# A two-block model on one core: the router's first scores taken tile by tile, and rows of U gathered two groups ahead of V

## The chip, the core and the metric

The kernel runs on one core of one Trainium2 chip. Its engines each run their own instruction stream: TensorE (PE, with its weight loads as PEld), VectorE (DVE), ScalarE (ACT), GpSimd (POOL) and SyncE (SP), and they wait for one another through semaphores. The metric is the device time of one execution in microseconds.

## The reference

The model is a block with two attention branches and a PEER layer, then two layers of a second block (gated linear attention beside latent attention). The change lies in the PEER layer and in the router ahead of it, for 256 tokens of width 1024:

```python
q = (hf @ wq).reshape(T, 8, 2, 128)                  # 8 heads, two halves each
sc = jnp.einsum('thpd,pnd->thpn', q, subkeys)        # 128 scores for each half
top_v, top_i = lax.top_k(sc, 16)
cand_v = top_v[:, :, 0, :, None] + top_v[:, :, 1, None, :]
best_v, best_j = lax.top_k(cand_v.reshape(T, 8, -1), 16)
ids = ...                                            # 128 rows of the tables for each token
gates = jax.nn.softmax(best_v, axis=-1)
a = jnp.einsum('td,ted->te', xb, jnp.take(u_tab, ids, axis=0))
w = gates * jax.nn.gelu(a, approximate=False)
y = jnp.einsum('te,ted->td', w, jnp.take(v_tab, ids, axis=0))
```

Each token takes 128 rows of U and the same 128 rows of V, each of 1024 float32 values. Both tables have 16384 rows and stay in HBM.

## The kernel before

**The PEER layer.** The tokens lie in two tiles of 128 (t = 0, 1). A *piece* is two heads of one tile, so there are 8 pieces. A piece has 32 row numbers for each token; 8 of them are a *group*, so there are 4 groups in a piece (GPP) and 32 in all. One gather is an indirect DMA that POOL issues: for each of the 128 partitions it fetches the row that this token wants, 512 KB. There are 256 gathers of U and 256 of V (`u_rows`, `v_rows`, both through L707). Rows of U go to 8 buffers (`urow`, half of the ring of weights), rows of V to 8 others (`vgat`). A row of U is used by one DVE instruction (L1786), which multiplies it with the token's activations and sums; this frees the buffer (`u_free`). After 8 rows ACT takes the gelu (L915), DVE multiplies with the gates (L1789), and ACT writes 8 diagonal matrices (L920). PE multiplies each diagonal with a row of V, two halves of 512 columns (L1317), into two banks that stay open for a whole tile; this frees the buffer of V (`v_free`).

**The order of the gathers.** `piece` (L724) issues for each group n the pairs U(n+1, s), V(n, s) for s = 0 to 7. So U runs one group ahead. The row numbers of a group are first copied to two small tiles (`stage_ids`, L711). U(n+1, s) waits until DVE has used U(n, s), V(n, s) until PE has used V(n-1, s).

**The selection.** For each piece DVE runs `best_halves` (16 best of each half), `best_pairs` (16 best of the sums) and `experts_and_gates` (row numbers and gates), for piece k+1 while piece k is gathered: one step after each of the first three groups; in the first piece the first step follows group 1, the other two group 2. ACT takes the exponentials of the gates (L910) between the last two.

**The router.** The order on PE and ACT is written out in `router_schedule` (L174). A job ("pq", ch) is the product with 512 columns of `peer_wq` (4 heads' halves), ("sc", t, ch) the scores of tile t against the subkeys from it; each takes whole PSUM banks, which `plan_banks` deals out in turn, and ACT empties them. Ahead of them the normalised rows of both tiles are transposed ("hT"). ("ada", 11) is the last of twelve products that spread a modulation vector over the partitions; DVE sums it first (`sum_ada`, L1531) and the product reads a tile of ones that lies in the space of `gates`. The first product, ch = 0, is made tile by tile (`tile_products`, L1117), so that it can begin while tile 1 is still normalised, but into banks that hold both tiles. Its scores feed the first selection, which ends in the first row numbers, for which POOL waits. The gathers also wait for the ring of weights: U(0, 0) for `sum_ada(11)`, U(0, 4) for ("pq", 1), V(0, 0) for ("pq", 2), V(0, 4) for ("pq", 3).

Ahead of the first selection DVE has this (L1773 to L1777):

```python
await_full(dve, ("ada", 11))
drained(dve, ("sc", 0, 0))
best_halves(0)
```

## Time and profile before

| | us |
|---|---|
| median of 3 runs | 1359.54 |
| lowest and highest | 1354.93, 1366.68 |
| the profiled execution | 1348.18 |
| its span in the trace | 1346.4 |
| DVE busy in the span | 645.3 (48%) |
| POOL busy in the span | 631.6 (47%) |
| PE busy in the span | 1074.0 (80%) |

The profiled execution is one of its own, and it is faster than each of the three timed runs. The gathers and their products fill the span from 262 to 1037 us. What lies ahead of them is the first block's attention and the router, and behind them the two layers of the second block. In rows of a timeline the first number is the start in us from the span's start and the second the duration in us.

### The profile page before, as it was taken

The page shows a single profiled execution, that of the slowest core. Times are in us where ns is not written, and L with a number is a line of the kernel's source. Part 1 is how long each engine was busy: PE and PEld are TensorE (multiplying, and loading weights), DVE is VectorE, ACT ScalarE, POOL GpSimd, SP SyncE. Part 2 cuts the span into 40 slices and gives each one's busy share as a digit, 9 for nine tenths or more (in the row PEclk, how much of TensorE's full clock was granted, in tenths as well). Part 3 has the DMA queues.
Part 4 walks back from the last instruction along what each step waited for, and adds up shares of the span by engine and source line. Part 5 has one row for each costly group of instructions (what it writes and reads, how often), then busy time and mean ns, then how long its engine had stood idle before and what let it go on. Part 6 is the DMA issues. An engine that isn't in the chain of part 4 may idle for free.

```text
span 1346.4 us, 11936 instructions
## 1 busy us (share of the span) xinstructions
PE 1074.0 (80%) x3367; PEld 544.1 (40%) x3367; DVE 645.3 (48%) x1463; ACT 269.2 (20%) x731; POOL 631.6 (47%) x653
## 2 busy tenths in 40 slices
PE   2899998997766667766776767766768999999988
PEld 2758655872222222222222222222224645555453
DVE  4534665557566465465555655564442133211530
ACT  3012231122011020110111311020111162113340
POOL 1400001177777777777777777777773001000000
PEclk9799999999999999999989799899999999799999
DMA  9985545499999999999999999999999543123300
GB/s 347 295 301 196 187 156 155 170 329 356 356 349 350 344 336 347 355 362 342 351 339 342 345 345 371 340 361 356 357 359 367 196 152 109 41 101 125 125 0 31
DMA packets 121589, 361.66 MB, mean 269 GB/s; under 512 B 13416, under 2 KB 16240, under 8 KB 121424
## 3 DMA queue, kind: packets, MB, share of 16 engines
q0 software_dynamic: 76000, 276.39, 56.6%
q1 hardware_dynamic: 42768, 82.97, 17.2%
q10 hardware_dynamic: 2784, 1.88, 0.5%
q8 instruction: 15, 0.25, 0.1%
q14 instruction: 22, 0.18, 0.0%
HBM read 360.15 MB, written 1.05 MB: 268 GB/s over the span
## 4 chain that ended last, share of the span: by engine, by line
PE 39%; POOL 21%; issue 17%; DMA 13%; ACT 5%; DVE 3%; POOLq 1%; ACTq 0%; DVEq 0%
POOL wring L707 21%; PE bank L1126 13%; DMA wring<-in_peer_v,small 9%; PE bank L1136 8%; PE bank L1317 5%; PE bank L1117 3%; DMA wring<-in_peer_u,small 3%; PE bank L1183 2%; PE bank L1197 1%; DVE R L1561 1%; DMA xrow<-in_x 1%; PE bank L1220 1%; PE bank L1474 1%; PE bank L1473 1%; PE bank L1306 1%
## 5 line engine op out<-in xcount | busy, mean ns | idle before, releaser
L1317 PE MATMUL bank<-wring,hT 128*128 128x512 f32 x1024 | 525.2, 642 | 214.7 <-DMA wring<-in_peer_v,small 213.3
L1786 DVE CUSTOM_DVE_ANT_0 wring<-wring,hrow 128x1024 f32<-128x1024 f32 x256 | 310.0, 1225 | 287.5 <-DMA wring<-in_peer_u,small 287.3
L1317 PEld LDWEIGHTS bank<-wring,hT 128*128 128x128 f32 x1024 | 183.2, 197 | 556.4 <-issue 518.4
L707 POOL DMA_INDIRECT wring<-in_peer_u,small x256 | 283.9, 1109 | 96.4 <-issue 59.1
L707 POOL DMA_INDIRECT wring<-in_peer_v,small x256 | 283.9, 1109 | 80.2 <-issue 74.2
L1126 PE MATMUL bank<-wring,hT 128*128 128x512 f32 (+1 forms) x448 | 195.3, 593 | 0.0
L745 POOL TENSOR_SCALAR small<-small 128x2 f32<-128x2 f32 (+3 forms) x16 | 3.1, 194 | 386.5 <-ACTq L817 220.8
L1126 PEld LDWEIGHTS bank<-wring,hT 128*128 128x128 f32 x448 | 85.1, 192 | 101.5 <-issue 101.5
L915 ACT ACTIVATE small<-small 128x8 f32<-128x8 f32 x32 | 6.7, 209 | 580.7 <-DVE small L1786 580.7
L1136 PE MATMUL bank<-hT,wring 128*128 128x256 f32 x448 | 101.9, 388 | 0.9 <-DVE hT L1578 0.9
L1136 PEld LDWEIGHTS bank<-hT,wring 128*128 128x128 f32 x448 | 86.2, 194 | 15.4 <-issue 3.6
L920 ACT ACTIVATE hT<-const,small 128x128 f32<-128x128 f32 x256 | 78.3, 388 | 11.4 <-DVE small L1789 11.4
L1117 PE MATMUL bank<-hT,wring 128*128 128x128 f32 x384 | 45.9, 282 | 8.4 <-ACT hT L840 8.4
L1531 DVE SCALAR_TENSOR_TENSOR modb<-wring,small,modb 128x512 f32<-128x512 f32 x64 | 48.1, 751 | 7.2 <-DMA wring<-in_ada_w 3.6
L1117 PEld LDWEIGHTS bank<-hT,wring 128*128 128x128 f32 x384 | 44.8, 197 | 9.8 <-issue 6.8
L711 POOL COPY small<-ids 128x8 uint32 (+1 forms) x64 | 16.1, 251 | 37.7 <-DVEq L1765 31.5
L1856 DVE SCALAR_TENSOR_TENSOR R<-R,small,gains 128x128 f32<-128x128 f32 x4 | 1.4, 348 | 57.7 <-POOLq L751 57.7
L2016 DVE TENSOR_TENSOR xrow<-xrow,bank 128x512 f32<-128x512 f32 x8 | 5.5, 688 | 48.6 <-PE bank L1126 48.6
L1183 PE MATMUL bank<-wring,hT 128*128 128x512 f32 x64 | 28.2, 596 | 0.3 <-ACT hT L870 0.3
L840 ACT ACTIVATE hT<-bank 128x512 f32<-128x512 f32 x24 | 13.5, 595 | 70.9 <-PE bank L1105 61.4
L685 POOL DMA_DIRECT2D hrow<-in_na_rpb x8 | 5.5, 720 | 45.9 <-DVE rope L1606 45.9
L892 ACT ACTIVATE R<-R,small 128x256 f32<-128x256 f32 x32 | 16.0, 500 | 42.1 <-DVEq L1660 42.1
(249 smaller groups left out, 883.9 us busy)
## 6 DMA issues: line engine op xcount, KB each, us to landing
wring<-in_w_in SPq DMA_DIRECT2D x14, 2048.0 KB, 9.4
wring<-in_ada_w SPq DMA_DIRECT2D x8, 2048.0 KB, 11.0
wring<-in_w_out SPq DMA_DIRECT2D x6, 2048.0 KB, 11.1
wring<-in_ada_w SPq DMA_DIRECT2D x8, 1024.0 KB, 16.2
wring<-in_peer_wq SPq DMA_DIRECT2D x4, 2048.0 KB, 12.0
wring<-in_peer_u,small POOLq DMA_INDIRECT x256, 6.1
wring<-in_peer_v,small POOLq DMA_INDIRECT x256, 6.2
wring<-in_w_in SPq DMA_DIRECT2D x2, 1792.0 KB, 14.8
```

Source lines behind the costliest of these rows:

```text
L707: pool.indirect_dma_start(dst, None, table, bass.IndirectOffsetOnAxis(index, 0)).then_inc(landed, 16)
L711: chain.link(pool.tensor_copy(dst, ids[:, bass.ds(n * GROUP, GROUP)] if not isinstance(n, int) else ids[:, n * GROUP:(n + 1) * GROUP]))
L840: free(act.activation(hT[:, 4 * g:4 * g + 4, t * P:(t + 1) * P], quad(pb[:, :]), ACT.Copy), (kind, t, g))
L892: act.activation(Em[:, h % 2, qt, :], Tm[:, h % 2, qt, :], ACT.Exp, scale=-1.0, bias=accmin[:, i:i + 1], accum_out=rsum[:, qt, h:h + 1]).t ...
L920: act.activation(diag[:, b * GROUP + s, :], ident, ACT.Copy, scale=w8[:, b, s:s + 1]).then_inc(diag_ready, 1)
L1117: last = pe.matmul(pb[:, o:o + P], w[:, k, a:a + P], hT[:, k, t * P:(t + 1) * P], start=k == 0, stop=k == KD - 1)
L1126: last = pe.matmul(pb[:, 0:n], hT[:, k, t * P:(t + 1) * P], w[:, k, wcol:wcol + n], start=k == 0, stop=k == KD - 1)
L1136: last = pe.matmul(pb[:, i * S:(i + 1) * S], w[:, k, a:a + P], hT[:, k, :], start=k == 0, stop=k == KD - 1)
L1183: last = pe.matmul(pb[:, :], hT[:, k, t * P:(t + 1) * P], w[:, k, :], start=k == 0, stop=k == KD - 1)
L1317: last = pe.matmul(pb[half][:, :], diag[:, b * GROUP + s, :], vgat[:, s, half * 512:(half + 1) * 512], start=False, stop=False, skip_group ...
L1531: ins = dve.scalar_tensor_tensor(acc, w[:, k, :], csil[:, k:k + 1], before, ALU.mult, ALU.add)
L1786: dve.tensor_tensor_reduce(urow[:, s, :], urow[:, s, :], hrow[:, t, :], 1.0, 0.0, ALU.mult, ALU.add, a8[:, b, s:s + 1]).then_inc(u_free, 1)
```

## The change

- `router_schedule` now begins with the transposes of the subkeys ("skT") and those of tile 0. ("first", t) takes the place of ("pq", 0): it is the same product, but for one tile alone, into one bank of its own for each tile (`first_heads`). The scores of tile 0 stand between the two. ("ada", 11) comes after ("first", 1). ("sc", 0, 1), the scores of the second piece, come ahead of ("pq", 3).
- POOL gathers all rows of U of groups 0 and 1, and then the pairs U(n+2, s), V(n, s). The last two groups of V stand alone.
- ACT's `peer_group` is split in `gelu` and `diagonals`. The first gelu stands between the evictions of ("pq", 1) and ("pq", 2), the second ahead of those of ("pq", 3), and the first diagonals after these.
- DVE runs the last two steps of the selection in one go after a piece's second group; in the first piece all three, and it waits there for the scores ("sc", 0, 1) alone.

```diff
@@ -173,9 +173,8 @@
 
 def router_schedule():
 
-
-    return [("pq", 0), ("sc", 0, 0), ("pq", 1), ("pq", 2), ("pq", 3)] + [
-        ("sc", t, ch) for ch in range(4) for t in range(NT) if (t, ch) != (0, 0)]
+    return ([("skT",), ("hT", 0), ("first", 0), ("hT", 1), ("sc", 0, 0), ("first", 1), ("ada", 11), ("pq", 1), ("pq", 2),
+             ("sc", 0, 1), ("pq", 3), ("sc", 1, 0), ("sc", 1, 1)] + [("sc", t, ch) for ch in (2, 3) for t in range(NT)])
 
...
@@ -577,9 +569,9 @@
         for job in ([("ada", i) for i in range(4)]
                     + [("qk", 0, 1), ("qk", 1, 1), ("ada", 4), ("v", 2, 1), ("qk", 3, 1), ("ada", 5), ("ada", 6),
                        ("qk", 4, 1), ("ada", 7), ("v", 5, 1), ("ada", 8), ("ada", 9), ("y", 0, 1), ("y", 1, 1),
-                       ("pq", 0, 1), ("ada", 10), ("ada", 11), ("pq", 1, 1), ("pq", 2, 1), ("pq", 3, 1)]):
-            w = {"ada": ada_w, "qk": w_in, "v": w_in, "y": w_out, "pq": peer_wq}[job[0]]
-            W1.append((w, 512 * (ADA[job[1]] if job[0] == "ada" else job[1]), job))
+                       ("first", 1), ("ada", 10), ("ada", 11), ("pq", 1, 1), ("pq", 2, 1), ("pq", 3, 1)]):
+            w = {"ada": ada_w, "qk": w_in, "v": w_in, "y": w_out, "pq": peer_wq, "first": peer_wq}[job[0]]
+            W1.append((w, 512 * (ADA[job[1]] if job[0] == "ada" else 0 if job[0] == "first" else job[1]), job))
         W1_AT = {job: n for n, (_, _, job) in enumerate(W1)}
         CPL = 8
         W1_USES = len(W1) // 4
@@ -724,15 +716,15 @@
             def piece(n, k, first=False, last=False):
 
                 for b in range(GPP):
-                    more = not (last and b == GPP - 1)
+                    more = not (last and b >= GPP - 2)
                     if more:
-                        if b == GPP - 1:
+                        if b == GPP - 2:
                             pool.wait_ge(ids_ready, k + 2)
-                        stage_ids(idu[:, (b + 1) % 2, :], n + b + 1)
+                        stage_ids(idu[:, b % 2, :], n + b + 2)
                     stage_ids(idv[:, b % 2, :], n + b)
                     for s in range(GROUP):
                         if more:
-                            u_rows(n + b + 1, s, (b + 1) % 2)
+                            u_rows(n + b + 2, s, b % 2)
                         if first and b == 0 and s % (GROUP // 2) == 0:
                             await_full(pool, ("pq", 2 + s // (GROUP // 2), 1))
                         v_rows(n + b, s, b % 2, first and b == 0)
@@ -766,6 +758,9 @@
                 if s == GROUP // 2:
                     await_full(pool, ("pq", 1, 1))
                 u_rows(0, s, 0, first=True)
+            stage_ids(idu[:, 1, :], 1)
+            for s in range(GROUP):
+                u_rows(1, s, 1)
             piece(0, 0, first=True)
             with pool.Fori(1, PIECES - 1) as k:
                 chain.loop(k - 1, 2 * GPP)
@@ -898,48 +893,64 @@
             norm_heads(1)
             ada_out(10)
             evac_oT(1)
-            for t in range(NT):
-                act.wait_ge(x_ready, t + 1)
-                squares([xrow[:, t, :]], [t])
-            evac_T("hT")
-            ada_out(11)
-
             def exponentials_of_gates(k):
                 act.wait_ge(softmax_shift, k + 1)
                 wait_alone(act)
                 act.activation(shifted, shifted, ACT.Exp).then_inc(gate_exp, 1)
 
 
-            def peer_group(n, b, first=False):
+            def gelu(n, b):
                 act.wait_ge(u_free, (n + 1) * GROUP)
                 act.activation(g8[:, b, :], a8[:, b, :], ACT.Gelu).then_inc(gelu_ready, 1)
+
+            def diagonals(n, b, first=False):
                 act.wait_ge(weights_ready, n + 1)
                 for s in range(GROUP):
                     if not first:
                         act.wait_ge(v_free, (n - 2) * GROUP + s + 1)
                     act.activation(diag[:, b * GROUP + s, :], ident, ACT.Copy, scale=w8[:, b, s:s + 1]).then_inc(diag_ready, 1)
 
+            def square_rows(t):
+                act.wait_ge(x_ready, t + 1)
+                squares([xrow[:, t, :]], [t])
+
+            square_rows(0)
             for job in router_schedule():
-                if job[0] == "pq":
+                if job[0] == "hT":
+                    evac_T("hT", None, [job[1]])
+                    if job[1] == 0:
+                        square_rows(1)
+                elif job[0] == "first":
+                    pb = await_full(act, job)
+                    free(act.activation(pqT[:, 0:4, job[1] * P:(job[1] + 1) * P], quad(pb[:, :]), ACT.Copy), job)
+                elif job[0] == "ada":
+                    ada_out(11)
+                elif job[0] == "pq":
                     ch = job[1]
+                    if ch == 3:
+                        gelu(1, 1)
                     for j in range(2):
                         pb = await_full(act, ("pq", ch, j))
                         i = 4 * ch + 2 * j
                         free(act.activation(pqT[:, i:i + 2, :].rearrange("p a b -> p (a b)"), pb[:, :], ACT.Copy), ("pq", ch, j))
-                        if (ch, j) == (3, 1):
-                            peer_group(0, 0, first=True)
                     if ch == 1:
                         exponentials_of_gates(0)
-                else:
+                        gelu(0, 0)
+                    if ch == 3:
+                        diagonals(0, 0, first=True)
+                elif job[0] == "sc":
                     _, t, g = job
                     pb = await_full(act, job)
                     free(act.activation(scores[:, 4 * t + g, :, :].rearrange("p a b -> p (a b)"), pb[:, :], ACT.Copy), job)
 
             def piece(k, first=False, last=False):
                 for b in range(GPP):
+                    n = k * GPP + b
+                    if not (first and b < 2):
+                        gelu(n, b % 2)
                     if not (first and b == 0):
-                        peer_group(k * GPP + b, b % 2, first and b < 2)
-                    if b == (2 if first else 1) and not last:
+                        diagonals(n, b % 2, first and b < 2)
+                    if b == 1 and not last:
                         exponentials_of_gates(k + 1)
 
             def norm_after(t):
@@ -1279,27 +1290,39 @@
                 full(last, ("skT",))
 
 
-            transpose_tile("hT", 0, 3 * NT)
+            def first_heads(t):
+
+                for g in range(2):
+                    drained(pe, ("hT", t, g))
+                w = weights1(pe, ("first", 1))
+                pb = claim(pe, ("first", t))
+                for i in range(4):
+                    for k in range(KD):
+                        last = pe.matmul(pb[:, i * P:(i + 1) * P], w[:, k, i * P:(i + 1) * P], hT[:, k, t * P:(t + 1) * P],
+                                         start=k == 0, stop=k == KD - 1)
+                full(last, ("first", t))
+
             for job in router_schedule():
-                if job[0] == "pq":
-                    ch = job[1]
-                    w = weights1(pe, ("pq", ch, 1))
-                    if ch == 0:
-
-                        for t in range(NT):
-                            if t > 0:
-                                transpose_tile("hT", t, 3 * NT)
-                            tile_products("hT", [("pq", 0, j) for j in range(2)], w, t)
-                        ada(11)
-                        transpose_subkeys()
-                    else:
-                        for j in range(2):
-                            columns_product(("pq", ch, j), w, j)
+                if job[0] == "skT":
+                    transpose_subkeys()
+                elif job[0] == "hT":
+                    transpose_tile("hT", job[1], 3 * NT)
+                elif job[0] == "first":
+                    first_heads(job[1])
+                elif job[0] == "ada":
+                    ada(11)
+                elif job[0] == "pq":
+                    w = weights1(pe, ("pq", job[1], 1))
+                    for j in range(2):
+                        columns_product(("pq", job[1], j), w, j)
                 else:
                     _, t, g = job
                     drained(pe, ("skT",))
-                    drained(pe, ("pq", g, 0))
-                    drained(pe, ("pq", g, 1))
+                    if g == 0:
+                        drained(pe, ("first", t))
+                    else:
+                        drained(pe, ("pq", g, 0))
+                        drained(pe, ("pq", g, 1))
                     pb = claim(pe, job)
                     for j in range(4):
                         i = 4 * g + j
@@ -1792,14 +1815,14 @@
             def piece(k, t, next_piece, first=False):
 
 
-                steps = {0: [best_halves], 1: [best_pairs], 2: [experts_and_gates]}
+                steps = {0: [best_halves], 1: [best_pairs, experts_and_gates]}
                 if first:
-                    steps = {1: [best_halves], 2: [best_pairs, experts_and_gates]}
+                    steps = {1: [best_halves, best_pairs, experts_and_gates]}
                 for b in range(GPP):
                     peer_group(k * GPP + b, b % 2, t)
                     for step in steps.get(b, []) if next_piece else []:
                         for job in router_schedule():
-                            if job[0] == "sc" and step is best_halves:
+                            if job[0] == "sc" and step is best_halves and (not first or job == ("sc", 0, 1)):
                                 drained(dve, job)
                         step(k + 1)
                 if next_piece:
```

PE in the router, as its instructions stand in the kernel before (`L1105` transposes hrow, `L1117` is `tile_products`, `L1149` ("ada", 11), `L1278` the subkeys, `L1306` scores, `L1136` the other products):

```order
L1105 MATMUL bank<-const,hrow 128x128 x8
L1117 MATMUL bank<-hT,wring 128x128 x32
L1105 MATMUL bank<-const,hrow 128x128 x8
L1117 MATMUL bank<-hT,wring 128x128 x32
L1149 MATMUL bank<-modb,gates 128x512
L1278 MATMUL bank<-const,skrow 128x128 x2
L1306 MATMUL bank<-skT,R 128x128 x4
L1136 MATMUL bank<-hT,wring 128x256 x96
L1306 MATMUL bank<-skT,R 128x128 x28
```

and after the change (`L1116` transposes hrow, `L1301` is `first_heads`, `L1160` ("ada", 11), `L1289` the subkeys, `L1329` scores, `L1147` the other products):

```order
L1289 MATMUL bank<-const,skrow 128x128 x2
L1116 MATMUL bank<-const,hrow 128x128 x8
L1301 MATMUL bank<-hT,wring 128x128 x32
L1116 MATMUL bank<-const,hrow 128x128 x8
L1329 MATMUL bank<-skT,R 128x128 x4
L1301 MATMUL bank<-hT,wring 128x128 x32
L1160 MATMUL bank<-modb,gates 128x512
L1147 MATMUL bank<-hT,wring 128x256 x64
L1329 MATMUL bank<-skT,R 128x128 x4
L1147 MATMUL bank<-hT,wring 128x256 x32
L1329 MATMUL bank<-skT,R 128x128 x24
```

The first scores moved from behind both tiles of the product, ("ada", 11) and the subkeys to a place between the tiles. ("ada", 11) still stands behind the second tile.

DVE ahead of the first selection, after the change: its waits (bank 4 is that of ("ada", 11), bank 2 that of ("sc", 0, 0), bank 0 that of the subkeys).

```order
L1554 SCALAR_TENSOR_TENSOR modb<-wring,small,modb 128x512 [waits dve_step,bank_full3,w_landed0]
L1554 SCALAR_TENSOR_TENSOR modb<-wring,small,modb 128x512 [waits dve_step] x7
L1731 COPY skT<-bank 128x256 [waits bank_full0]
L1796 MEMSET modb 128x1024
L1797 MEMSET pT 128x128
L1759 COPY R<-R 128x512 [waits bank_free2,dve_step,bank_full4]
L1742 MAX R<-R 128x8 [waits dve_step]
```

Before, the copy to `R` waited for banks 0 and 4, those of the same two jobs; the wait for ("ada", 11) has stayed.

POOL at the start of the gathers, before:

```order
L711 COPY small<-ids 128x8
L707 DMA wring<-in_peer_u,small 128x1024 x8
L711 COPY small<-ids 128x8 x2
L707 DMA wring<-in_peer_u,small 128x1024
L707 DMA wring<-in_peer_v,small 128x1024
L707 DMA wring<-in_peer_u,small 128x1024
L707 DMA wring<-in_peer_v,small 128x1024
```

and after the change:

```order
L703 COPY small<-ids 128x8
L699 DMA wring<-in_peer_u,small 128x1024 x8
L703 COPY small<-ids 128x8
L699 DMA wring<-in_peer_u,small 128x1024 x8
L703 COPY small<-ids 128x8 x2
L699 DMA wring<-in_peer_u,small 128x1024
L699 DMA wring<-in_peer_v,small 128x1024
L699 DMA wring<-in_peer_u,small 128x1024
L699 DMA wring<-in_peer_v,small 128x1024
```

Eight gathers of U were put in a row ahead of the first pair.

## Rows read from the trace of the kernel before

**Rows 1.** page, costliest groups: count | busy us, mean ns | idle before, releaser
```profile
L1786 DVE CUSTOM_DVE_ANT_0 wring<-wring,hrow 128x1024 f32<-128x1024 f32 x256 | 310.0, 1225 | 287.5 <-DMA wring<-in_peer_u,small 287.3
...
L707 POOL DMA_INDIRECT wring<-in_peer_u,small x256 | 283.9, 1109 | 96.4 <-issue 59.1
L707 POOL DMA_INDIRECT wring<-in_peer_v,small x256 | 283.9, 1109 | 80.2 <-issue 74.2
```

**Rows 2.** waits of POOL, 260 to 1060 us: total us, times, longest
```profile
POOL wring L707 <- PE bank L1317: 25.6, 58, 0.9
```

**Rows 3.** timeline of DVE, 224 to 261 us: ada 11, skT, first selection
```profile
224.67 6.26 DVE L1531 SCALAR_TENSOR_TENSOR modb<-wring,small,modb 128x512 f32<-128x512 f32 x8
...
241.40 0.42 DVE L1708 COPY skT<-bank 128x256 f32<-128x256 f32 x1 [10.48 <-PE bank L1278]
...
244.98 0.43 DVE L1736 COPY R<-R 128x512 f32<-128x512 f32 x1 [1.93 <-ACT R L936]
...
260.41 0.19 DVE L1763 SCALAR_TENSOR_TENSOR ids<-R 128x32 uint32<-128x32 f32 x1
```

**Rows 4.** timeline of PE in the router, 222 to 244 us
```profile
222.36 8.84 PE L1117 MATMUL bank<-hT,wring 128*128 128x128 f32 x64 [4.26 <-ACT hT L840]
...
232.90 7.38 PE L1117 MATMUL bank<-hT,wring 128*128 128x128 f32 x64 [0.83 <-ACT hT L840]
...
240.12 1.02 PE L1149 MATMUL bank<-modb,gates 128*128 128x512 f32 x2
...
243.01 1.13 PE L1306 MATMUL bank<-skT,R 128*128 128x128 f32 x8 [1.65 <-ACT R L928]
```

**Rows 5.** a window of PE: us, busy (x), granted clock, DMA share, GB/s
```profile
222.00:223.00 1.00, 0.64 (x3) 0.51 1.06 389
```

**Rows 6.** timeline of POOL: gathers 1, 6, 7 and 8 of 512
```profile
262.34 1.08 POOL L707 DMA_INDIRECT wring<-in_peer_u,small  x1 [0.95 <-POOL small L711]
...
269.16 1.91 POOL L707 DMA_INDIRECT wring<-in_peer_u,small  x1 [0.30 <-issue]
...
271.37 1.60 POOL L707 DMA_INDIRECT wring<-in_peer_u,small  x1 [0.30 <-issue]
...
273.28 1.28 POOL L707 DMA_INDIRECT wring<-in_peer_u,small  x1 [0.30 <-issue]
```

**Rows 7.** timelines of POOL and DVE: a gather, the reduction beside it
```profile
601.88 1.99 POOL L707 DMA_INDIRECT wring<-in_peer_u,small  x1 [0.31 <-issue]
...
601.84 1.22 DVE L1786 CUSTOM_DVE_ANT_0 wring<-wring,hrow 128x1024 f32<-128x1024 f32 x1
```

**Rows 8.** page, DMA issues: count, KB each, us to landing
```profile
wring<-in_peer_u,small POOLq DMA_INDIRECT x256, 6.1
```

**Rows 9.** timelines of DVE and POOL: selection steps, two group starts
```profile
333.10 1.22 DVE L1758 TENSOR_TENSOR R<-R,const 128x1024 f32<-128x1024 uint32 x1
...
337.86 1.22 DVE L1786 CUSTOM_DVE_ANT_0 wring<-wring,hrow 128x1024 f32<-128x1024 f32 x1
...
593.35 0.69 DVE L1743 TENSOR_TENSOR R<-R 128x512 f32<-128x512 f32 x1
...
599.54 1.22 DVE L1786 CUSTOM_DVE_ANT_0 wring<-wring,hrow 128x1024 f32<-128x1024 f32 x1
...
588.80 0.96 POOL L707 DMA_INDIRECT wring<-in_peer_u,small  x1 [0.88 <-POOL small L711]
...
613.27 0.96 POOL L707 DMA_INDIRECT wring<-in_peer_u,small  x1 [0.89 <-POOL small L711]
```

**Rows 10.** timeline of POOL and PE at the end of the gathers
```profile
1016.45 0.96 POOL L707 DMA_INDIRECT wring<-in_peer_v,small  x1 [0.84 <-POOL small L711]
...
1020.84 16.07 PE L1317 MATMUL bank<-wring,hT 128*128 128x512 f32 x36 [0.58 <-DMA wring<-in_peer_v,small]
...
1036.74 1.88 PE L1333 MATMUL bank<-hrow,pT 128*128 128x512 f32 x4
```

19 lines of the change are left out of this document (6 added, 13 removed).

## The prediction, written before the changed kernel ran

> **What bounds the kernel now.** I read the page first. The 512 gathers fill over half of the span, and no engine is fully busy in them, so the page alone does not name the bound. Its groups show POOL at 283.9 + 283.9 = 567.8 us in the instructions that issue gathers, 1.109 us each, and DVE's reduction of a row of U at 310.0 us in all [rows 1]. Next came POOL's timeline. Between two gathers lie 0.30 us whatever came before [rows 6]. From the first gather at 262.34 to the 505th at 1016.45 pass 754.1 us for 504 gathers, 1.50 us each [rows 6, 10]; 1.11 + 0.30 of that is POOL's own issuing, and the rest are mostly the copies of the row numbers. Last came the waits. POOL's largest wait for another engine's buffers while it gathers is 25.6 us in 58 pieces, none over 0.9 us [rows 2]. That is 0.44 us each, barely more than the 0.30 between any two gathers. So **POOL's issuing sets the pace**, and it does not wait for free buffers.
>
> A gather that nothing holds up takes 0.96 us [rows 9, 10], the mean one 1.109. The excess is 567.8 - 512 x 0.96 = 76 us, 0.30 us for each of the 256 reductions. Its cause can be seen: the gather at 601.88 lasts 1.99 us and ends 0.81 us after the reduction beside it has ended, 603.87 against 603.06 [rows 7]. A gather that begins while DVE reduces waits for the end of that reduction. What this change can move is therefore the time of the first gather, the copies and the hold-ups of POOL, any new wait of POOL, and what follows the last gather. How far U runs ahead of V is in itself worth nothing here.
>
> **The start.** Before, the first selection began at 244.98 [rows 3], behind both tiles of the first product. After, the scores of tile 0 need the copy of the subkeys, and that stands on DVE behind the sum for ("ada", 11), which ends at 224.67 + 6.26 = 230.93; with 0.42 for the copy the scores can start at 231.4 [rows 3]. PE has been idle by then: tile 0's product can begin near 219 (PE waited 4.26 us for ACT, which now empties tile 0's transposes first) and takes 7.4 us, the transposes about 1. Then the scores 1.13, tile 1's product, and ("ada", 11) 1.02 [rows 4]. The selection still waits for that last one. The product of a tile took 7.38 us, but 8.84 us after the idle 4.26 us, when the granted clock was 0.51, the lower of its two levels, 1.2 GHz [rows 4, 5]. The idle time ahead of the scores is about as long, so I take 8.84: 231.4 + 1.13 + 8.84 + 1.02 = 242.4, and 242.5 with the hand-over. The gain is **-2.5 us**; with 7.38 it is -3.9. The scores' early place alone would have given over 10 us; the wait for ("ada", 11) takes most of it. The selection itself is unchanged: 15.4 us from its first row to the row numbers [rows 3].
>
> **Eight rows of U alone.** Now 16 gathers of U stand in a row, and each lands beside a reduction. The trace has such a stretch: gathers 6 to 8 begin at 269.16, 271.37 and 273.28, and the last takes 1.28 + 0.30, which is 1.90 us each [rows 6] against 0.96 + 0.30 = 1.26 unhindered. That is 0.64 us of hold-up for a row where the mean is 0.30. Eight more: 8 x 0.34 = **+2.7 us**. The bounds are a hold-up of nothing, 8 x -0.30 = -2.4, and the 1.99 us of rows 7 every time, 8 x 0.73 = +5.8. I take the nearest row, which is the same instruction in the same place.
>
> The Trainium skill ("SBUF — State Buffer", Who interferes with whom) says that a DVE instruction with two SBUF inputs holds up a GpSimd instruction that reads SBUF, but infers that descriptor generation is not held up by it. The gather of rows 7 shows the gather held up all the same. By the page's inference this term and the burst below would be nothing, and the sum 3.7 us less.
>
> **Three steps in one.** In the first piece DVE runs the whole selection after group 1. By the pace above, gather 8 ends at 272.1 and gather 16 begins near 286.7; it lands 6.1 us later [rows 8], its reduction (1.2) ends at 294.0, gelu and gates add 0.6, the selection 16.4 (244.98 to the gates just behind 260.41 + 0.19 [rows 3]), so group 2's first row is reduced at 312.2. POOL wants to put U(3, 0) into its place after 16 more gathers, near 311.1. **+1 us**, between 0 and 2. Eight rows then wait for DVE, which takes them back to back in 9.8 us; POOL gets a gather through every 1.99 + 0.30 us, so 4 of them are held up by 1.03 us [rows 7]: 4.1 us where 8 x 0.30 = 2.4 is usual. Before there was half such a burst. **+1 us**.
>
> ACT now holds the evictions of ("pq", 3) until gelu 1, near 294.6. Behind them stand two jobs of scores of 1.13 us on PE, so V's first product comes near 300. V(1, 0) is not issued before 312, which hides it. SP's loads for ("pq", 2) and ("pq", 3) now wait for the end of tile 1's product, as before, about 1 us later; the product ("pq", 1) covers them.
>
> **The steady state.** Pairs take 599.54 - 593.35 = 6.2 us, experts and gates 337.86 - 333.10 = 4.8 [rows 9], together 11.0. They begin 4.6 us after the group's first gather (588.80 to 593.35), so the next group's first reduction ends at 4.6 + 11.0 + 1.2 = 16.8 us, and its buffer is wanted after 24.5 (588.80 to 613.27 [rows 9]). The slack of 7.7 us hides it. The longer pause makes a longer burst, but one instead of two, for the same number of pauses' microseconds: 0. ACT's diagonals of group n now wait for PE to use V of group n-2, some 3 us after the gates are ready; only the exponentials stand behind them, and these wait 6.2 us for the pairs anyway: 0. The number of copies and gathers is the same: 0, but for half a microsecond.
>
> **The end.** The last 16 rows of V now come alone. Before, 8 did: the first was issued at 1016.45, and PE took the last 9 rows in 16.07 us, 1.79 each [rows 10], slower than POOL issues them. So PE sets the end from the landing of the first lone row, 1020.84 + 1.79 = 1022.6, 6.2 us after its issue. After, that row is issued 8 x 1.26 = 10.1 us earlier, lands at 1012.5, and 16 x 1.79 = 28.6 us follow: 1041.1 against 1036.9. **+4.2 us**; at least +2 if some landings overlap better, at most +6. SP's loads for the next layer hang on the sixth product from the end, as before.
>
> **Sum:** -2.5 + 2.7 + 1 + 1 + 4.2 = **+6.4 us**. The profiled execution, 1348.2, would become 1354.6. It lies 11.4 us under the median of the three timed runs, 1359.5; against that median, which the new time will be held against, the forecast is 1366, slower by 0.5%. A change under 1% (13.6 us) cannot be told from none here, since the three runs themselves spread over 11.8 us.
>
> **Rivals.**
>
> *The start wins (16%).* Clock high in tile 1's product (-3.9), U alone held up no more than usual (0), no burst or stall, the end +2: -2 us, 1358. For it speaks that the first gather took 1.08 us [rows 6], against it that gathers 6 to 8 did not run so. It stays within 1%.
>
> *POOL did wait for buffers (6%).* If the 25.6 us [rows 2] were true waits for rows of V, an earlier gelu and diagonals would remove them: 1366 - 25.6 = 1340. Against it: the pieces are of 0.30 and 0.9 us, the same as where nothing is waited for.
>
> *The hold-ups change phase, slower (12%).* Whether a gather is held up depends on tenths of a microsecond between its start and DVE's. If the new order of steps moves the mean hold-up from 0.30 to 0.36 us for a row or more, the 256 rows cost 15 us on top: 1381. It decides once about 15 more of the 512 gathers are caught for a full 1.03 us. For it: longer bursts, in which every gather is caught. Against it: in the steady state the alternation of U and V, the latency and the reduction all stay.
>
> *The same, faster (3%):* 15 us less, 1351.
>
> *DVE's combined step makes POOL wait in every piece (3%).* It needs 7.7 us more than the 11.0 us; then each microsecond beyond costs 7 pieces one each, 1373 and more.
>
> The forecast has the other 60%. The range takes the start between -3.9 and -2.5, U alone from -2.4 to +5.8, the end from +2 to +6, some 6 us of spread of the runs to each side, and reaches to both phase rivals' near sides: 1351 to 1380. The forecast's own part is 1358 to 1373. Faster by over 1%, under 1346: 0.08. Within 1%: 0.76. Slower by over 1%, over 1373: 0.16.
>
> **What would show it.** The first reduction's start and POOL's first gather: 259.8 if the start is right, near 252 if the wait for ("ada", 11) had not mattered. POOL's starts of gathers 9 to 16: 1.9 us apart, or 1.26. A wait of POOL for DVE at the 33rd gather. POOL's mean gather: 1.11 us again; 1.14 would be the slower phase rival, and POOL's waits for PE gone the faster one. The stretch from the last lone pair to PE's last product: 29 us with PE without a gap. The forecast is wrong if the steady pace per 32 gathers, 48 us before, moves by over half a microsecond.

## The result

The changed kernel took 1373.7 us (median of 4 runs, 1371.0 to 1386.6) against 1363.1 for the kernel before (4 runs beside them, 1354.9 to 1369.7): ratio 1.0139, 95% interval 1.0088 to 1.0191. The forecast was 1366 within 1351 to 1380, and "within 1%" with a chance of 0.76. The time fell into the range, but the loss was 10.6 us and not 6.4: over 1%, the case that I had given 0.16. A time in us is the median of a whole series, while a ratio compares on each side only the runs within 1.5% of that side's fastest, so the two need not divide out.

Two more series of the same changed kernel, below, gave 1.0048 and 1.0027. Weighted by their intervals the three make 1.0061, some 8 us. They differ among themselves by more than their intervals allow, and so does the kernel before against itself (0.9964 in one series). **One series here is good to about half a per cent, whatever its interval says**; the experiments are therefore read in pairs, several pairs for one question. The later series were run in five batches, each on a chip of its own with the kernel before in it.

### The profile page after: what moved, and what is told of

Read it like the earlier page. It is cut to its first block, busy times and chain, and to the rows that moved or that the text cites. A ratio compares the mean times of both kernels' runs of the same rounds, so it can differ in the third digit from the quotient of the medians.

```text
span 1374.4 us, 11986 instructions
## 1 busy us (share of the span) xinstructions
PE 1087.6 (79%) x3367; PEld 550.2 (40%) x3367; DVE 645.6 (47%) x1463; ACT 269.3 (20%) x731; POOL 641.0 (47%) x653
## 4 chain that ended last, share of the span: by engine, by line
PE 35%; POOL 22%; issue 20%; DMA 9%; DVE 7%; ACT 4%; another core or an unknown queue 1%; POOLq 1%; DVEq 0%; ACTq 0%
POOL wring L699 21%; PE bank L1137 13%; DMA wring<-in_peer_v,small 6%; PE bank L1340 5%; PE bank L1147 4%; PE bank L1128 2%; DMA wring<-in_peer_u,small 2%; PE bank L1194 2%; PE bank L1208 1%; DVE R L1584 1%; DMA xrow<-in_x 1%; PE bank L1231 1%; PE bank L1497 1%; POOL small L703 1%
## 5 line engine op out<-in xcount | busy, mean ns | idle before, releaser
L1340 PE MATMUL bank<-wring,hT 128*128 128x512 f32 x1024 | 534.7, 653 | 225.5 <-DMA wring<-in_peer_v,small 201.6
L1340 PEld LDWEIGHTS bank<-wring,hT 128*128 128x128 f32 x1024 | 186.9, 201 | 572.2 <-issue 558.8
L699 POOL DMA_INDIRECT wring<-in_peer_u,small x256 | 288.5, 1127 | 107.6 <-issue 68.4
L1137 PEld LDWEIGHTS bank<-wring,hT 128*128 128x128 f32 x448 | 85.3, 193 | 102.1 <-issue 102.1
L1147 PE MATMUL bank<-hT,wring 128*128 128x256 f32 x448 | 100.8, 385 | 0.9 <-DVE hT L1601 0.9
L1147 PEld LDWEIGHTS bank<-hT,wring 128*128 128x128 f32 x448 | 85.3, 192 | 15.5 <-issue 4.1
L1554 DVE SCALAR_TENSOR_TENSOR modb<-wring,small,modb 128x512 f32<-128x512 f32 x64 | 48.1, 751 | 7.7 <-DMA wring<-in_ada_w 4.1
L703 POOL COPY small<-ids 128x8 uint32 (+1 forms) x64 | 20.0, 312 | 34.9 <-DVEq L1788 28.8
L1128 PE MATMUL bank<-hT,wring 128*128 128x128 f32 x256 | 29.6, 276 | 3.0 <-ACT hT L835 3.0
L1128 PEld LDWEIGHTS bank<-hT,wring 128*128 128x128 f32 x256 | 28.9, 192 | 3.9 <-ACT hT L835 3.9
L1194 PE MATMUL bank<-wring,hT 128*128 128x512 f32 x64 | 28.2, 596 | 0.3 <-ACT hT L865 0.3
```

Source lines behind the costliest of these rows:

```text
L699: pool.indirect_dma_start(dst, None, table, bass.IndirectOffsetOnAxis(index, 0)).then_inc(landed, 16)
L703: chain.link(pool.tensor_copy(dst, ids[:, bass.ds(n * GROUP, GROUP)] if not isinstance(n, int) else ids[:, n * GROUP:(n + 1) * GROUP]))
L1128: last = pe.matmul(pb[:, o:o + P], w[:, k, a:a + P], hT[:, k, t * P:(t + 1) * P], start=k == 0, stop=k == KD - 1)
L1137: last = pe.matmul(pb[:, 0:n], hT[:, k, t * P:(t + 1) * P], w[:, k, wcol:wcol + n], start=k == 0, stop=k == KD - 1)
L1147: last = pe.matmul(pb[:, i * S:(i + 1) * S], w[:, k, a:a + P], hT[:, k, :], start=k == 0, stop=k == KD - 1)
L1194: last = pe.matmul(pb[:, :], hT[:, k, t * P:(t + 1) * P], w[:, k, :], start=k == 0, stop=k == KD - 1)
```

## The profile after, beside the rows of before

DVE, PE and POOL in the router, timelines of the changed kernel, columns as in [rows 3, 4, 6]:

```profile
225.12 6.25 DVE L1554 SCALAR_TENSOR_TENSOR modb<-wring,small,modb 128x512 f32<-128x512 f32 x8
...
231.29 0.42 DVE L1731 COPY skT<-bank 128x256 f32<-128x256 f32 x1
...
242.65 0.43 DVE L1759 COPY R<-R 128x512 f32<-128x512 f32 x1 [9.72 <-PE bank L1160]
...
258.09 0.19 DVE L1786 SCALAR_TENSOR_TENSOR ids<-R 128x32 uint32<-128x32 f32 x1
```

```profile
231.77 1.16 PE L1329 MATMUL bank<-skT,R 128*128 128x128 f32 x8 [3.95 <-DVE skT L1731]
232.76 8.94 PE L1301 MATMUL bank<-hT,wring 128*128 128x128 f32 x64
241.53 1.02 PE L1160 MATMUL bank<-modb,gates 128*128 128x512 f32 x2
```

Here L1329 are the scores, L1301 the second tile's product and L1160 ("ada", 11). The start is as forecast step by step: scores behind the copy of the subkeys at 231.8 (231.4), the second tile's product in 8.94 us (8.84) after 3.95 us of idle PE, then ("ada", 11), and the selection at 242.65 (242.5).

```profile
260.01 1.08 POOL L699 DMA_INDIRECT wring<-in_peer_u,small  x1 [0.94 <-POOL small L703]
...
273.27 1.70 POOL L699 DMA_INDIRECT wring<-in_peer_u,small  x1 [0.83 <-POOL small L703]
...
285.38 1.61 POOL L699 DMA_INDIRECT wring<-in_peer_u,small  x1 [0.30 <-issue]
...
288.65 1.08 POOL L699 DMA_INDIRECT wring<-in_peer_u,small  x1 [0.83 <-POOL small L703]
...
319.48 1.17 POOL L699 DMA_INDIRECT wring<-in_peer_u,small  x1 [9.27 <-DVE small L1809]
```

Gathers 1, 9, 16, 17 and 33. The first is 2.3 us earlier. Gathers 9 to 16 start (285.38 - 273.27) / 7 = 1.73 us apart, so that the 17th is 1.7 us later than before. Then POOL waits 9.27 us at the 33rd gather, where I had foreseen 1. DVE shows why:

```profile
300.88 0.42 DVE L1745 FIND_INDEX8 R<-R 128x8 uint32<-128x256 f32 x1
302.43 0.41 DVE L1748 MATCH_REPLACE8 R<-R 128x256 f32<-128x256 f32 x1
302.83 0.41 DVE L1748 MATCH_REPLACE8 R<-R 128x256 f32<-128x256 f32 x1
305.22 0.75 DVE L1751 MAX8 R<-R 128x8 f32<-128x256 f32 x2 [1.99 <-remote]
...
311.58 0.19 DVE L1771 TENSOR_TENSOR R<-R 128x32 f32<-128x32 f32 x1 [4.04 <-remote]
...
578.73 0.87 DVE L1751 MAX8 R<-R 128x8 f32<-128x128 f32 x4 [5.11 <-remote]
583.77 0.09 DVE L1754 MATCH_VALUE_LOAD R<-R 128x8 f32 x1 [4.16 <-remote]
...
679.00 0.87 DVE L1751 MAX8 R<-R 128x8 f32<-128x128 f32 x4 [6.85 <-remote]
684.59 0.09 DVE L1754 MATCH_VALUE_LOAD R<-R 128x8 f32 x1 [4.72 <-remote]
```

Inside the selection DVE stands still for 2 to 7 us, on instructions that depend only on DVE's own results; "remote" means that the profile found no releaser. There are seven such stops, 28.8 us together. The first selection in one go took 317.54 - 292.96 = 24.6 us instead of the 16.4 of [rows 3]. POOL's waits over the same stretch as [rows 2] (total us, times, longest), of the changed kernel:

```profile
POOL wring L699 <- PE bank L1340: 25.6, 36, 4.6
...
POOL wring L699 <- DVE small L1809: 9.3, 1, 9.3
```

POOL's pauses over a microsecond, of which before had a single one of 1.98 us, add up to 22.5 us beyond the 0.30 that lies between any two gathers. That is most of the 27.25 us by which the peer stage ended later in this profile (1063.99 against 1036.74 [rows 10]). Three of them follow stops of DVE, at the 33rd, 209th and 272nd gather, and are 15.5 us longer than the idle time usual at their place. The groups of the page, against [rows 1]:

```profile
L1809 DVE CUSTOM_DVE_ANT_0 wring<-wring,hrow 128x1024 f32<-128x1024 f32 x256 | 308.4, 1224 | 279.1 <-DMA wring<-in_peer_u,small 267.8
...
L699 POOL DMA_INDIRECT wring<-in_peer_u,small x256 | 288.5, 1127 | 107.6 <-issue 68.4
L699 POOL DMA_INDIRECT wring<-in_peer_v,small x256 | 284.9, 1113 | 88.8 <-issue 79.9
```

The end, PE's timeline against [rows 10]:

```profile
1034.71 29.45 PE L1340 MATMUL bank<-wring,hT 128*128 128x512 f32 x68 [0.59 <-DMA wring<-in_peer_v,small]
1063.99 1.88 PE L1356 MATMUL bank<-hrow,pT 128*128 128x512 f32 x4
```

This is 17 rows of V at 1.73 us without a gap: the stretch of 29 us was forecast. Whether it costs anything is another question, answered below.

## The experiments

Each was timed in five rounds beside the kernel before. Ratios are to before, with 95% intervals.

**1. The changed kernel again, twice.** Are DVE's stops the code's, or one execution's? No edit.

> The changed kernel once more, without an edit. In its first profile VectorE stood still for 1 to 7 us at a time inside its selection steps, with nothing to wait for that its waits show: 8.4 us in the first selection in one go (33rd gather at 319.48 instead of 310.10), and 5 to 12 us at a time after groups 12 and 16; the kernel before has none of these in its one profile. Theory A, these stops belong to the changed code (the steps in one go, or the place of VectorE's code): the new profile shows the first one again, the 33rd gather at 319 +-1.5 us, and the ratio to before is 1.010 to 1.018. Theory B, they are the luck of one execution: the first stop is gone, the 33rd gather stands at 311 to 313, and the ratio comes out at 1.003 to 1.008, as the terms of the prediction gave it.

> The changed kernel a third time, without an edit. Its two series gave 1.0139 and 1.0048 to before; pooled 1.008. Expected 1.005 to 1.012. If VectorE's stops (51.6 us in the first profile, none in the second) belong to the changed code, this profile has a good chance of some again; if they are rare luck, none, and first to last gather 766 to 773 us.

1360.1 us, ratio 1.0048 (1.0007 to 1.0088), and 1360.7 us, 1.0027 (0.9987 to 1.0067), the second below its expected 1.005. Neither profile has one stop of DVE over 0.6 us in a selection. POOL's 33rd gather in the first of them:

```profile
311.77 0.38 POOL L703 COPY small<-ids 128x8 uint32<-128x8 uint32 x1
312.31 0.98 POOL L703 COPY small<-ids 128x8 uint32<-128x8 uint32 x1 [0.17 <-POOL small L703]
314.13 1.10 POOL L699 DMA_INDIRECT wring<-in_peer_u,small  x1 [0.83 <-POOL small L703]
```

No wait beyond the usual 0.83 us behind a copy, but 314.13 is 4.0 us behind before and a microsecond later than theory B had it. The stops belonged to one execution. First gather to last took 770.9 and 780.7 us (766 to 773 were expected), 793.8 with the stops.

**2. The change taken apart.** Three kernels. "one_ahead" is the changed kernel with POOL's order of before (without the eight rows of group 1 ahead, and with the gelu of group 1 back behind the router, since that group's rows now come later); cut:

```diff
-                    more = not (last and b >= GPP - 2)
+                    more = not (last and b == GPP - 1)
-                        if b == GPP - 2:
+                        if b == GPP - 1:
-                        stage_ids(idu[:, b % 2, :], n + b + 2)
+                        stage_ids(idu[:, (b + 1) % 2, :], n + b + 1)
```

> The changed kernel with POOL's order of before: rows of U one group ahead, POOL's wait for the experts' numbers at a piece's last group; the router, and VectorE's three steps in one go, stay. Theory A (the steps in one go are what stops VectorE and POOL behind it): the steps' stop is there, but POOL now waits for the numbers only 16 pairs later, so its 33rd gather is not late; about 1365 us, ratio 1.000 to 1.006. Theory B (the price is the 16 lone rows of U ahead and of V behind, 2.7 and 4.2 us in the prediction): 7 us below the changed kernel, 1364 to 1367 us, ratio 1.000 to 1.004. Theory C (the loss is in the router's new order, which moves ScalarE's and TensorE's other work under the gathers): as slow as the changed kernel, ratio 1.012 or more.

1358.8 us, 1.0054 (1.0023 to 1.0084), in theory A's range, above B's, far below C's. "router_only" is before with the router's new order alone; the first gelu and the steps stand as before:

> The kernel before with the router's new order alone (by tile, a bank of its own for the first scores, ada chunk 11 after the second tile's product); gathers one group ahead, selection steps and gelu as before. The first gather was 2.3 us earlier in the changed kernel and I found nothing that the new order costs later: 1360 to 1362 us, ratio 0.997 to 1.000. Theory C (the router's new order is what costs): ratio above 1.005. Theory A or B: not above 1.001.

1346.8 us, 0.9990 (0.9949 to 1.0030), as expected: theory C falls. "gathers_only" is before with the lead of two groups and the steps in one go:

> The kernel before with the gathers two groups ahead and the steps in one go alone; the router as before. By the prediction's terms: start 0, lone rows of U +2.7, stall 1 and burst 1, end +4.2, so +9 us, ratio 1.006 to 1.007, 1372 us. Theory A (VectorE's stops belong to the steps in one go): another 8 to 15 us, ratio 1.012 to 1.018, and the profile shows POOL waiting for VectorE 8 us or more at its 33rd gather. Theory C (the router costs): ratio below 1.006.

1368.0 us, 1.0138 (1.0076 to 1.0199; 6 runs). Its profile shows POOL waiting 2.9 us at the 33rd gather, not 8. It shows another wait, which the changed kernel does not have, on DVE and then on POOL:

```profile
289.38 0.17 DVE L1792 TENSOR_TENSOR small<-small,gates 128x8 f32<-128x8 f32 x1 [8.78 <-ACT small L918]
```

```profile
291.50 1.18 POOL L707 DMA_INDIRECT wring<-in_peer_u,small  x1 [4.52 <-PE bank L1309]
```

This kernel kept ACT's order of before, in which the first gelu stands behind the evictions of ("pq", 3). DVE waits 8.78 us for it with the rows of group 1 landed behind it, and POOL loses 3.7 us beyond the usual at the 17th gather. So gathers_only is not the changed kernel less its router: it also lacks the early gelu, and part of its loss is that.

The router's order is free; the loss is in the other parts.

**3. The steps in one go alone, and all three in one go.** On the kernel before (cut; in the first piece all three steps stand together behind group 1, and the exponentials follow them):

```diff
-                steps = {0: [best_halves], 1: [best_pairs], 2: [experts_and_gates]}
+                steps = {0: [best_halves], 1: [best_pairs, experts_and_gates]}
```

> The kernel before with one edit: best_pairs and experts_and_gates in one go after a piece's second group (and all three in one go in the first piece); gathers one group ahead and the router as before. Theory A (the long step is paid in every piece: after it VectorE does six reductions back to back instead of three, and each holds up the gather beside it; the group of 16 gathers behind the step took 25.0 to 25.3 us instead of 24.0 in the two kernels with the two orders together, 24.8 in the one with gathers one ahead): +1.2 us a piece, 7 pieces, +5 to +9 us, ratio 1.004 to 1.007. Theory B (the prediction's: the step's slack of 7.7 us covers it, steady state 0; the loss of the kernel with gathers one ahead was in the router's order of ScalarE's work): ratio 0.998 to 1.002.

1357.1 us, 1.0067 (1.0030 to 1.0104): theory A's number. Yet its one profile shows the peer stage ending 2.9 us earlier than before's, and POOL's 512 gathers taking 7 us less than before's: the profile does not show the loss.

All three steps in one go in every piece:

```diff
-                steps = {0: [best_halves], 1: [best_pairs], 2: [experts_and_gates]}
+                steps = {1: [best_halves, best_pairs, experts_and_gates]}
```

> The kernel before with all three selection steps in one go after every piece's second group, 19.6 us of VectorE at a stretch (8.1 + 6.3 + 5.1) in place of 11.4 in the changed kernel and 8.1 in the kernel before: the suspected cost, made larger. Theory A (reductions back to back behind a long step hold up the gathers beside them): eight back to back, +2 us or more a piece, ratio 1.010 to 1.018, with the group of 16 gathers behind the step at 26 us or more. Theory B (the transfers make the pace and the step's delay is given back in the next group): ratio 0.998 to 1.004, the group behind the step longer and the next ones shorter.

1373.0 us, 1.0159 (1.0125 to 1.0194). The mean group of 16 gathers behind the step took 26.9 us (before: 24.2), with 7.1 gathers over 1.2 us in it (before: 4.0), and of the 2.6 us more the other three groups of a piece gave back a third. But POOL now waits for DVE as well (waits of POOL, total, times, longest):

```profile
POOL wring L707 <- PE bank L1317: 29.6, 54, 4.3
POOL wring L707 <- DVE small L1786: 14.3, 7, 3.3
```

So the cost grows with the step: none is seen with the steps apart, 8.1 us of DVE the longest, 9 us in all with 11 us, 22 us with 19.6. This is not one cause made larger: first gather to last took 19 us longer than before, of which 12.4 are waits of POOL for buffers that the long step kept, 3.3 the gathers themselves and 3.4 the copies.

**4. The steps of before in the changed kernel, twice.** The reverse of 3:

```diff
-                steps = {0: [best_halves], 1: [best_pairs, experts_and_gates]}
+                steps = {0: [best_halves], 1: [best_pairs], 2: [experts_and_gates]}
                 if first:
-                    steps = {1: [best_halves, best_pairs, experts_and_gates]}
+                    steps = {1: [best_halves], 2: [best_pairs, experts_and_gates]}
```

> The changed kernel with the selection in the three steps of before (halves, pairs, experts after a piece's first three groups; in the first piece halves after the second, pairs and experts after the third); gathers two ahead, POOL's wait for the numbers at a piece's third group, router and gelu as changed. By the profile the numbers are there about 13 us into the 24 us of POOL's second group, so that POOL need not wait. Theory A (the steps in one go cost 5 to 9 us): ratio 0.999 to 1.004. Theory F (the lead of two groups itself is what costs, 16 lone rows at either end and held-up gathers): as the changed kernel, 1.006 to 1.011.

> The same kernel as three_steps, a second time. Theory A (the steps in one go cost the changed kernel 7 to 10 us): again 0.996 to 1.003. If it comes out at 1.004 or above, the first series was lucky and the steps' share is under 5 us.

1350.5 us, 0.9989 (0.9955 to 1.0022), and 1352.4 us, 1.0006 (0.9963 to 1.0049). The numbers are ready in time with the steps apart: POOL's 33rd gather starts 0.83 us behind its copy in both profiles. The one wait of 1.9 us, at the 114th gather, comes with the longer lead: the changed kernel's profiles have 2.0, 1.0 and 1.3 us there. Putting the steps together was not needed for the lead, and it is what cost.

**5. The steps spread otherwise.** Halves of the piece after next behind a piece's last group (cut; DVE's loop over the second tile's pieces is written out in this kernel):

```diff
+                steps = {0: [(best_pairs, 1)], 1: [(experts_and_gates, 1)], 3: [(best_halves, 2)]}
```

> The changed kernel with its selection steps apart: halves of the piece after next after a piece's last group, pairs after its first, experts after its second (in the first piece halves after the first group, pairs and experts after the second); POOL still finds the numbers ready at a piece's third group. Theory A (the long step is paid in every piece): 5 to 8 us below the changed kernel, and its first piece's wait of POOL at the 33rd gather gone too; against before ratio 1.001 to 1.004, and no group of 16 gathers above 24.5 us in the mean. Theory B (the steps cost nothing): as the changed kernel, ratio 1.005 to 1.012.

1360.3 us, 1.0086 (1.0046 to 1.0125): theory A missed, and the number is theory B's. The groups of 16 gathers came down to 24.4 us at most in the mean, but waits of POOL of 3.3, 1.8 and 5.0 us stand in its profile, the last at the change of tile. These waits are its only excess that the profile shows; where a step stands matters too.

**6. What it is that a long step does.** On before, behind every group's weights, the same DVE time with and without passes of two inputs:

```diff
+                for i in range(3):
+                    dve.tensor_tensor_reduce(region(11264 + 1024 * i, 1024), hrow[:, t, :], hrow[:, t, :], 1.0, 0.0, ALU.mult, ALU.add,
+                                             R[:, 10600 + i:10601 + i])
```

```diff
+                for i in range(9):
+                    dve.max(R[:, 12288 + 8 * i:12296 + 8 * i], hrow[:, t, 0:256])
```

> The kernel before with three more reductions behind every group's weights, two inputs of 128 x 1024 each read from a resident row (hrow with itself) and written to spare room: 3.5 us more of VectorE a group of 16 gathers, 32 groups. Theory A (a two-input pass of VectorE holds up the gather beside it): 96 more passes at the 0.34 us that each of before's 256 costs POOL (86.6 us over 0.94 us a gather, of 512 gathers) make +33 us of POOL at most, +15 to +35 us, ratio 1.011 to 1.026, POOL's mean gather at 1.15 to 1.18 us instead of 1.11. Theory B (only the lateness of the reductions counts, and these come where VectorE has 3 to 10 us to spare): ratio 0.998 to 1.004.

> The same place and nearly the same VectorE time (nine maxima of 128 x 256 from one input, 0.38 us each, 3.4 us a group) without a two-input pass. Theory A: nothing, ratio 0.998 to 1.003, mean gather 1.11 us. If the lateness alone counts, the same as the kernel with more reductions. If any VectorE work holds up gathers, 1.01 or more as well.

1400.5 us, 1.0359 (1.0312 to 1.0406), and 1374.7 us, 1.0170 (1.0124 to 1.0216). Both are above what I expected, and the maxima were to cost nothing. Page groups, first with more reductions, then with more maxima:

```profile
L707 POOL DMA_INDIRECT wring<-in_peer_u,small x256 | 317.9, 1242 | 96.4 <-issue 63.4
L707 POOL DMA_INDIRECT wring<-in_peer_v,small x256 | 290.0, 1133 | 80.3 <-issue 75.8
```

```profile
L707 POOL DMA_INDIRECT wring<-in_peer_u,small x256 | 292.3, 1142 | 96.4 <-issue 58.5
L707 POOL DMA_INDIRECT wring<-in_peer_v,small x256 | 292.8, 1144 | 80.3 <-issue 75.2
```

A gather with only the added maxima beside it took 0.937 us (64 of them in the second kernel), as long as one with nothing beside it (0.945); one beside a reduction took 1.24 in the mean. So maxima hold up nothing themselves. They delay the reductions behind them, which then more often stand back to back: 61 reductions came third or later in an unbroken run, against 27 before, and the gathers took 17.3 us more with no reduction added. POOL's waits for DVE stayed at 0.3 us. The added reductions delay the others as much, so of the 40.1 us that they put on the gathers only the 22.8 us beyond the maxima's are the price of the 96 passes themselves. The Trainium skill ("SBUF — State Buffer", Who interferes with whom) says that a DVE instruction with at most one SBUF input does not contend with GpSimd; the 0.937 us agree.

What decides is when a gather begins. In the profile of before 229 gathers began while a reduction ran and took 1.30 us in the mean; of the 146 beside which a reduction began only later, all but one took their usual time, 0.945 in the mean. In more_maxima the two are 210 at 1.39 and 107 at 0.938: 149 gathers took over 1.0 us where before had 147, but they were caught earlier in a reduction, so that each waited longer.

**7. The start without its wait.** On the changed kernel, chunk 11 behind the first scores, the subkeys' copy ahead of DVE's sum:

```diff
-("sc", 0, 0), ("first", 1), ("ada", 11), ("pq", 1)
+("sc", 0, 0), ("ada", 11), ("first", 1), ("pq", 1)
```

> The changed kernel with the wait that it kept at the start taken out: ada chunk 11 directly behind the first scores and ahead of the second tile's product, and the copy of the sub-keys ahead of VectorE's sum for chunk 11. Theory D (the product of the second tile, 9 us, stands between the first scores and the selection only by its place ahead of ada 11): selection starts at 234 to 236 instead of 242.7 to 244.7, first gather near 252, and 6 to 8 us less than the changed kernel, ratio to before 0.999 to 1.004. Theory E (rows of V wait for the room that the later products free, so that an earlier start is handed back): first V gather no earlier than now, under 2 us gained, ratio 1.005 to 1.01.

1352.4 us, 1.0013 (0.9973 to 1.0054). Timeline of DVE, then of POOL:

```profile
226.06 0.42 DVE L1730 COPY skT<-bank 128x256 f32<-128x256 f32 x1
226.39 6.25 DVE L1554 SCALAR_TENSOR_TENSOR modb<-wring,small,modb 128x512 f32<-128x512 f32 x8
...
233.99 0.43 DVE L1759 COPY R<-R 128x512 f32<-128x512 f32 x1
```

```profile
251.35 1.08 POOL L699 DMA_INDIRECT wring<-in_peer_u,small  x1 [0.94 <-POOL small L703]
```

The selection starts 8.7 us earlier, 233.99, and so does the first gather. The first row of V is issued at 277.57 instead of 290.04 and waits for nothing new (theory E falls).

**8. Together.** "all_three" joins 7, 5 and a last piece in which V's rows catch up, three to two of U's; "early_three_steps_end" has the steps of before in place of 5; "early_three_steps" is that without the catching up.

```diff
+                    while us and 2 * GROUP - len(us) < 2 * (b * GROUP + s + 1) / 3:
+                        g, r = us.pop(0)
```

> The changed kernel with three edits: the early start (chunk 11 behind the first scores), the selection steps apart, and the last piece's rows of V gathered three for every two of U, so that one group of V remains alone at the end and not two. If the terms hold and add up: -7 (start), -6 (steps) and -3 (end) from the changed kernel's 1360, so 1344 us, ratio to before 0.993 to 0.997. If the room for rows of V binds at the start (theory E) ratio 0.998 to 1.002. If the end is bound by something other than the 16 lone rows of V, the time from the last gather to the end of the peer products stays at 14 us but the last gather is not earlier.

> The changed kernel with the early start (chunk 11 behind the first scores), the three steps of before, and the last piece's rows of V three to every two rows of U. If the long step costs as theory A says, this loses what all_three lost to its steps behind a piece's last group (5.0 us of waiting at the change of tile, 5.8 us at its first selection): 1336 to 1343 us, ratio 0.991 to 0.997. Theory F: ratio 0.998 to 1.002.

> The same kernel as early_three_steps_end, a second time. It gave 0.9918 (0.988 to 0.996) to before; expected 0.989 to 0.996, and below 1 if the gain is one.

> early_three_steps_end without its third edit: two groups of V remain alone at the end, as in the changed kernel. By the prediction's term (8 more lone rows at 1.79 us of TensorE instead of 1.24 us of POOL or 1.5 us of the loop's pace) 2.3 to 4.4 us more than with the edit: ratio 0.994 to 0.996. If the end costs nothing, as early_three_steps_end, 0.992.

all_three: 1348.8 us, 1.0009 (0.9974 to 1.0044), above its expected 0.993 to 0.997, with waits of 5.8 us at the first selection and 5.0 at the change of tile, as in 5. early_three_steps_end: 1342.7 us, 0.9918 (0.9879 to 0.9957), and again 1341.2 us, 0.9927 (0.9887 to 0.9967). early_three_steps: 1339.9 us, 0.9940 (0.9909 to 0.9971). **These three series are 6 to 8 per mille below the kernel before.** What the catching up adds, 2 us, is inside the noise; its PE stretch at the end, from the kernel's second series, has 10 rows and not 17:

```profile
1013.35 17.48 PE L1349 MATMUL bank<-wring,hT 128*128 128x512 f32 x40 [0.57 <-DMA wring<-in_peer_v,small]
1030.66 1.88 PE L1365 MATMUL bank<-hrow,pT 128*128 128x512 f32 x4
```

**The kernel before, again,** for the scatter:

> The kernel before once more, without an edit, for a second profile and for how well two series of one kernel agree. Ratio 0.996 to 1.004. Its time from the first gather to the last was 764.5 us in the first profile; theory A (the long step costs 5 to 9 us in the pace) needs it at 760 to 768 again, and needs steps_only's 760.1 us, which shows no loss, to have been a lucky execution.

1349.7 us, 0.9964 (0.9929 to 0.9999); first gather to last 766.2 us.

## Why the prediction was partly wrong

Pairs that differ in one part (and in places of the first gelus) tell what each part is worth, in ratios to before:

| part | pairs (with the part, without) | difference | forecast |
|---|---|---|---|
| steps in one go | 1.0067, 1 · 1.0054, 0.9990 · 1.0061, 0.9996 · 1.0013, 0.9940 | +0.0067, +0.0064, +0.0065, +0.0073 | +2 us, 0.0015 |
| lead of two groups | 1.0138, 1.0067 · 1.0061, 1.0054 · 0.9996, 0.9990 | +0.0071, +0.0007, +0.0006 | +6.9 us, 0.0051 |
| router's order | 0.9990, 1 · 1.0054, 1.0067 · 1.0061, 1.0138 | -0.0010, -0.0013, -0.0077 | -2.5 us, -0.0018 |

(1.0061 and 0.9996 are the means of the changed kernel's and of three_steps' series.) If one series is good to half a per cent, one difference is good to 0.007 and the mean of four to 0.0035: that the four of the first row agree to 0.001 is partly luck, and what they show is +9 us, give or take 5. The odd last figure of the bottom row and first of the middle one both rest on gathers_only, which waits for its late gelu.

**The start, -2.5: right,** in place and size (the timed pairs, -0.0010 and -0.0013, are too coarse to tell). Over all profiles the first gather stood at 264.2 us in the mean of 7 kernels with the old router and at 261.4 in the mean of 8 with the new.

**Eight rows of U alone, +2.7: seen, and made up for later.** They came 1.73 us apart, the 17th gather 1.7 us later although the first was 2.3 earlier (+4.0). But the rest of the loop made it up: first gather to last took 764.5 and 766.2 us with before's lead, 766.6, 764.3 and 766.5 with the lead of two, the steps apart and 16 lone rows at the end.

**The end, +4.2: too much.** From the 481st gather to the end of the peer products passed 55.8 and 59.2 us in two profiles before, 56.9 in the mean of the five profiles with 8 lone rows (before's two, router_only, one_ahead, steps_only), and 57.2 to 59.5, mean 58.4, in the nine with 16: +1.5 us, less than before's two differ. Both terms together came to 0.0007 of the time in the two pairs without gathers_only, 1 us, where 6.9 stood; the timed pairs alone would not exclude 6.9, but the profiles say the same as they.

**The steps in one go, +2 and "0" in the steady state: this failed.** I wrote: "The longer pause makes a longer burst, but one instead of two, for the same number of pauses' microseconds: 0." Four pairs say +0.0064 to +0.0073, 9 us. The slack of 7.7 us held, in so far as POOL waited for no row of U in a later piece of the two undisturbed profiles. What was put at nothing is the burst, which the same prediction had priced at +1 us in the first piece. Behind the step DVE now does six reductions in a row instead of three; DVE's and POOL's timelines in the third profile of the changed kernel:

```profile
602.42 1.22 DVE L1809 CUSTOM_DVE_ANT_0 wring<-wring,hrow 128x1024 f32<-128x1024 f32 x1
...
603.57 1.22 DVE L1809 CUSTOM_DVE_ANT_0 wring<-wring,hrow 128x1024 f32<-128x1024 f32 x1
...
604.72 1.22 DVE L1809 CUSTOM_DVE_ANT_0 wring<-wring,hrow 128x1024 f32<-128x1024 f32 x1
```

```profile
601.32 1.99 POOL L699 DMA_INDIRECT wring<-in_peer_v,small  x1 [0.30 <-issue]
603.62 1.99 POOL L699 DMA_INDIRECT wring<-in_peer_u,small  x1 [0.30 <-issue]
605.91 0.93 POOL L699 DMA_INDIRECT wring<-in_peer_v,small  x1 [0.30 <-issue]
606.84 0.78 POOL L703 COPY small<-ids 128x8 uint32 x1
```

In such a run a reduction starts every 1.15 us, and a gather caught for the full 1.99 + 0.30 us spans two of them, so every second reduction of the run catches one. From the third on a reduction costs POOL 0.5 to 0.7 us in the mean, where one that stands alone costs 0.30. Before had 27 third or later ones, the changed kernel 44 and 43 in its two profiles without stops. The group of 16 gathers behind the step took 25.2 and 25.4 us there, where before took 24.1. The other three groups of a piece gave back a part of it.

Whether this burst makes the 9 us is not shown. The time from the first gather to the last splits into the gathers, the copies of the row numbers and POOL's waits beyond the idle time usual at their place (0.30 us, or 0.84 behind a copy), each the mean over profiles, in us:

| | gathers | copies | waits | first to last |
|---|---|---|---|---|
| three steps, six profiles | 565.7 (562.6 to 568.7) | 17.1 | 2.9 | 765.7 (764.3 to 766.6) |
| pairs and experts together, six without stops | 566.3 (558.0 to 576.8) | 19.7 | 4.0 | 770.0 (760.1 to 780.7) |
| the changed kernel with its stops | 572.5 | 19.8 | 21.3 | 793.8 |

(The first row leaves out early_three_steps_end, whose last piece has another order: 773.6 and 769.2.) Without the stops the kernels with the long step are 4.3 us slower, half of what the timed pairs say, and the gathers make 0.6 us of it; steps_only and start_early, with 49 and 50 reductions third or later, spent less on gathers than any kernel with three steps. The six spread over 21 us instead of 2. So the long step is shown to cost, by the timed pairs; that the burst is the cause is argued from the group behind the step and from experiment 6, and which part of the 9 us is burst, copies, waits or stops like those of the first profile stays open. It is the third rival's direction, priced there at 15 us with 0.12, but its sign, a mean gather of 1.14 us, did not come in the mean.

**The sum** was 6.4 us and the pooled measurement is 8: near by luck, through two errors of opposite sign, 6 us too much for the lead and 7 too little for the steps. The first series, 10.6 us, has its profile with the stops among its four runs; no other kernel that was run again differs from itself by more than 0.004, this one by 0.011, and whether stops lengthened the other three runs is not known.

**The signs named ahead:** first gather 260.0 (259.8); 1.73 us between lone rows (1.9); the mean gather 1.127 and 1.113 us, then 1.104 and 1.112, then 1.142 and 1.115, or 1.120, 1.108 and 1.129 for U and V together, against the 1.11 of the forecast and the 1.14 of the rival. The pace from the 33rd to the 481st gather, per 32, was 48.05 us before and 49.2, 48.1 and 48.8 in the three profiles of the changed kernel, 47.8 and 47.6 with three steps: over half a microsecond in two of three (in one of them with the stops), the sign for "the forecast is wrong".
